# One-hots of the expert lookup in bfloat16 pairs, and the turn of the slot indices two pieces earlier

## The chip, the core and the metric

The kernel runs on one core of one Trainium2 chip, as one launch. Its time is device time in microseconds (us); the number compared is the median of repeated executions. Engines are named as the profile names them: PE (TensorE, matmuls; PEld its weight loads), DVE (VectorE), ACT (ScalarE), POOL (GpSimd), SP (which only issues DMAs here).

## The reference

Two transformer blocks run one after the other over 256 tokens of width 1024. The change touches one part, the product-key expert layer (PEER) that stands twice in the first block. For each token and each of 8 heads it finds the 16 best of 128 keys on each of two sides, adds them in pairs, keeps the 16 best pairs, and from the place of each pair it looks up which two keys made it:

```python
s = jnp.einsum('bthcd,hcnd->bthcn', q, sub_keys).astype(F32)
top_s, top_i = lax.top_k(s, PEER_TOPK)                       # 16 of 128, for both sides c
cand_s = (top_s[..., 0, :, None] + top_s[..., 1, None, :]).reshape(B, T, PEER_HEADS, -1)
cand_i = (top_i[..., 0, :, None] * PEER_NKEYS + top_i[..., 1, None, :]).reshape(B, T, PEER_HEADS, -1)
best_s, pos = lax.top_k(cand_s, PEER_TOPK)                   # 16 of 256 pairs
idx = jnp.take_along_axis(cand_i, pos, axis=-1)
gate = jax.nn.softmax(best_s, axis=-1)
...
h = jax.nn.gelu(jnp.einsum('md,mkd->mk', xb, exp_u[ib]), approximate=False)
return jnp.einsum('mk,mkd->md', (gb * h).astype(xb.dtype), exp_v[ib])
```

All 16384 experts are computed for all tokens by the kernel, and a table of gates (zero where an expert was not chosen) weighs them.

## The kernel before

All engines run programs written out by hand and meet at counted semaphores; the order within an engine is the order of the code. The expert layer (functions `peer_tensor`, `peer_scalar`, `peer_vector`, `load_peer`, once for each of the two layers) has 64 "pieces" of 256 experts, in two phases.

In the first phase, the h phase, piece c is 48 matmuls on PE (lines 1389 to 1391: two halves of 8 steps with three passes each, so that fp32r halves add up to full precision). Its weights come in raw by DMA; ACT rounds each half (`split_u`, L1539), DVE subtracts the rounded from the raw half (`residue_u`, L1634, two instructions of 128x1024 for a piece), and PE needs both. There are four buffers of half a piece, so DVE and ACT can be at most two pieces ahead of PE: the second residue of piece c waits for ACT, which waits until PE is through with piece c - 2. After each piece ACT applies the gelu (L1547), and after every fourth it also issues a store (L1550).

Beside this work, DVE chooses the experts, in stretches between residues. `between(work)` adds up given costs and puts in the two residues of the next piece when 24 is reached, and then counts from 0 again. First come the searches for the 16 best (L1651 to L1660). Then, four times (two token tiles n // 2, two sides n % 2), a one-hot of 128 pairs x 16 places is compared (L1689), multiplied by the 16 key numbers (L1693) and summed over the 16 places (L1695), all in fp32; that yields `slotI` and `slotJ`. Then the gates `slotG` are made (L1699 to L1701), one more piece of residues is put out, and DVE waits for PE to turn the three arrays (`turn_slots`, six transposes, L1454, which PE does after piece `SLOTS_AT` = 30). DVE copies the turned values as bfloat16 pairs (L1706 to L1713).

From piece `GATES_FROM` = 32 to `GATES_TO` = 60, 32 "groups" of 8 tokens are spread over the pieces by `groups_at`: DVE builds one-hots for a group (`one_hots`, five instructions of 128x1024 bfloat16, L1725 to L1730, in which each value stands twice in neighbouring places), PE multiplies them (24 matmuls, L1465), ACT copies the result out (L1559), and every fourth group is stored. With 28 pieces for 32 groups, pieces 32, 39, 46 and 53 have two groups. Before the groups of piece c, DVE has put out the residues of all pieces up to c + 1. The second phase, the y phase, begins when the gates have been stored and read back.

Of the kernel before, what the change touches and what calls it, by code (L numbers as in the profile page):

```python
# [7 lines left out]
ALU = mybir.AluOpType  # L8
ACT = mybir.ActivationFunctionType
AXX = mybir.AxisListType.X  # L10
F32 = mybir.dt.float32
U32 = mybir.dt.uint32
I32 = mybir.dt.int32
F32R = mybir.dt.float32r
BF16 = mybir.dt.bfloat16


P = 128
T = 256
TT = T // P  # L20
# [14 lines left out]
TOPK = 16  # L35
# [104 lines left out]
def two_blocks(nc, x, mem, consts, cols, rows, small, subk, wfix, peer, moe, gtab, ctab, kvtab, out):  # L140
# [23 lines left out]
    def A(off, *shape):  # L164

        n = 1
        for d in shape:
            n *= d
        v = arena[:, off:off + n]
        if len(shape) == 2:  # L170
            return v.rearrange("p (a b) -> p a b", a=shape[0])
        if len(shape) == 3:
            return v.rearrange("p (a b c) -> p a b c", a=shape[0], b=shape[1])
        return v
# [6 lines left out]
    def K(name, *shape):  # L181
        o, n = CONST[name]
        v = con[:, o:o + n]
        return v.rearrange("p (a b) -> p a b", a=shape[0]) if len(shape) == 2 else v
# [21 lines left out]
    def over(ap, axis, n):  # L206

        v = ap.unsqueeze(axis)
        s = list(v.shape)
        s[axis] = n  # L210
        return v.to_broadcast(s)

    def along(ap, n):

        return over(ap, len(ap.shape), n)
# [6 lines left out]
    def S(name):  # L222
        if name not in sems:
            sems[name] = nc.alloc_semaphore(name)
        return sems[name]
# [58 lines left out]
    def link(ins):  # L284

        dve_steps[0] += 1
        ins.then_inc(S("dve_step"), 1)
        nc.vector.wait_ge(S("dve_step"), dve_steps[0])
# [977 lines left out]
    s_sb = A(0, TT, 16, NKEYS)  # L1266
    cand = A(4096, TT, 8, 256)
    qTp = A(8192, 8, T)
    tv, ti, tif = A(10240, TT * 16, TOPK), A(10752, TT * 16, TOPK).bitcast(U32), A(11264, TT * 16, TOPK)
    bv, bp = A(11776, TT * 8, TOPK), A(12032, TT * 8, TOPK).bitcast(U32)  # L1270
    pa, pb = A(12288, TT, P), A(12544, TT, P)
    pau, pbu = (A(o, TT, P).bitcast(U32) for o in (15616, 15872))
    oneh = [A(12800, P, TOPK), A(4096, P, TOPK)]
    slotI, slotJ, slotG = (A(o, TT, P) for o in (14848, 15104, 15360))
    gsum = A(16128, TT * 8)
    slots_of = [A(16384 + 256 * n, T).bitcast(BF16).rearrange("p (t q) -> p t q", q=2) for n in range(4)]
# [3 lines left out]
    iota16 = A(23552, 64).bitcast(BF16).rearrange("p (k q) -> p k q", q=2)  # L1280
# [89 lines left out]
    BLOCK = JG // JC  # L1370
    NB = 4

    EXP_AT, SLOTS_AT, GATES_FROM, GATES_TO = 23, 30, 32, 60
    MEMORY_AT = 20

    def groups_at(c):
# [240 lines left out]
    def peer_vector(dve, l):  # L1617
# [10 lines left out]
        def residue_u():  # L1628

            nonlocal done  # L1630
            for j in range(JC):
                m = JC * (hb + done) + j
                dve.wait_ge(S("w1_hi"), m + 1)
                dve.tensor_tensor(u_lo[m % NB], u_raw(done, j), u_hi[m % NB].bitcast(F32), ALU.subtract)\  # L1634
                   .then_inc(S("w1_lo"), 1)
            done += 1

        def between(work):

            nonlocal spent  # L1640
            spent += work
            if spent >= 24:
                residue_u()
                spent = 0
# [20 lines left out]
        for tt in range(TT):  # L1665
# [1 line left out]
            w = slice(16 * tt, 16 * tt + 16)  # L1667
            top16(lambda i: s_sb[:, tt, i, :], tv[:, w], ti[:, w], 16, 2)
            dve.sem_inc(S("keys_best"), 1)
        link(dve.tensor_copy(tif, ti))  # L1670
        between(6)
        for tt in range(TT):
            w = slice(8 * tt, 8 * tt + 8)
# [6 lines left out]
        link(dve.tensor_scalar(pbu, bpf, TOPK - 1, None, ALU.bitwise_and))  # L1680
        dve.tensor_tensor(bv, bv, along(gsum, TOPK), ALU.subtract).then_inc(S("gate_in"), 1)
        known = done
        dve.tensor_copy(pa, pau)
        link(dve.tensor_copy(pb, pbu))
        between(12)

        tif5 = tif.rearrange("p (a c h) k -> p a c h k", a=TT, c=2)
        for n in range(4):
            link(dve.tensor_tensor(oneh[n % 2], along((pa, pb)[n % 2][:, n // 2, :], TOPK),  # L1689
                                   over(K("iota")[:, 0:TOPK], 1, P), ALU.is_equal))  # L1690
            between(16)
            o4 = oneh[n % 2].rearrange("p (h k) a -> p h k a", h=8)
            link(dve.tensor_tensor(o4, o4, over(tif5[:, n // 2, n % 2], 2, TOPK), ALU.mult))  # L1693
            between(16)
            link(dve.tensor_reduce((slotI, slotJ)[n % 2][:, n // 2, :], oneh[n % 2], AXX, ALU.add))  # L1695
            between(16)
        assert known - 1 <= EXP_AT <= done, (known, done)
        dve.wait_ge(S("gate_exp"), l + 1)
        link(dve.tensor_reduce(gsum, bv, AXX, ALU.add))  # L1699
# [5 lines left out]
        dve.wait_ge(S("slots_mm"), l + 1)  # L1705
        dve.tensor_copy(I2, along(ps[:, 6, 0:T], 2))  # L1706
        dve.tensor_copy(J2, along(ps[:, 6, T:2 * T], 2))
        dve.tensor_copy(iota16, K("iota").rearrange("p (k q) -> p k q", q=2))
        link(dve.tensor_copy(G1, along(ps[:, 7, 0:T], 2)))
        link(dve.tensor_tensor(g_left, ps[:, 7, 0:T], G1[:, :, 0], ALU.subtract))  # L1710
        link(dve.tensor_copy(G2, along(g_left, 2)))
# [1356 lines left out]
    with block_ctx as block:  # L3068
# [48 lines left out]
        @block.vector  # L3117
        def _(dve):
            even_vector(dve)
            peer_vector(dve, 0)  # L3120
            odd_vector(dve)
            peer_vector(dve, 1)
            mix2_vector(dve)
            xa_vector(dve)
            moe_vector(dve)
# [93 lines left out]
```

## Time and profile before

| | us |
|---|---|
| median of 3 executions | 3217.57 |
| lowest, highest | 3216.59, 3219.06 |
| profiled execution, device time | 3216.88 |
| span in its trace | 3215.1 |
| PE busy | 3012.1 (94%) |
| DVE busy | 2201.4 (68%) |
| ACT busy | 1496.7 (47%) |

The span is the time from the first to the last instruction in the trace; 1.8 us of the device time lie around it. Busy time counts instructions of an engine that overlap once. The two expert layers lie at about 340 to 1160 and 1364 to 2180 us.

### The profile page before, as it was taken

To read this page: it belongs to the slowest core of one execution; us is meant where nothing else is said; L and a number is where in the kernel's file an instruction comes from. 1 tells how busy PE (TensorE), PEld (TensorE's weight loads), DVE (VectorE), ACT (ScalarE), POOL (GpSimd) and SP (SyncE) were. 2 spreads that over 40 slices of the span, in tenths; PEclk is the share of its full clock that TensorE was granted. 3 is DMA by queue.
4 is the path that set the end of the run, shared out by engine and by line. 5 is a ranking of instruction groups with operands and counts; after the bars stand their busy time and mean duration, and the time that the engine had idled before them with its cause. 6 is when DMAs were issued, how large, how long until landed. Compare 5 with 4: busy or idle time off the path is not lost.

```text
span 3215.1 us, 41793 instructions
## 1 busy us (share of the span) xinstructions
PE 3012.1 (94%) x17215; PEld 2494.8 (78%) x17215; DVE 2201.4 (68%) x3375; ACT 1496.7 (47%) x1736; POOL 60.1 (2%) x94
## 2 busy tenths in 40 slices
PE   8898999999999998899899999998997799999995
PEld 4785898999888856499899988876545578888884
DVE  0654698776676646379777666666723488999996
ACT  1220344665545411144466544443121278888884
POOL 0000000000000000000000000000000000000000
PEclk9897999999999999899999999998998799999998
DMA  6102465677988733246577897862233189999994
GB/s 233 42 1 90 146 236 199 226 261 287 368 290 292 261 144 118 105 168 224 193 261 252 320 347 282 296 232 79 105 131 131 59 341 394 403 399 394 400 394 184
DMA packets 111838, 746.55 MB, mean 232 GB/s; under 512 B 9200, under 2 KB 42272, under 8 KB 48800
## 3 DMA queue, kind: packets, MB, share of 16 engines
q1 hardware_dynamic: 96064, 640.68, 53.6%
q10 hardware_dynamic: 8256, 73.23, 5.5%
q0 software_dynamic: 7328, 29.97, 2.4%
q8 instruction: 136, 2.23, 0.3%
q14 instruction: 54, 0.44, 0.0%
HBM read 655.23 MB, written 88.60 MB: 231 GB/s over the span
## 4 chain that ended last, share of the span: by engine, by line
PE 86%; DVE 10%; DMA 2%; ACT 2%; issue 1%; ACTq 0%; SPq 0%; POOL 0%; DVEq 0%; POOLq 0%
PE ps L1389 19%; PE ps L1390 19%; PE ps L1391 19%; PE ps L396 10%; PE ps L390 7%; PE ps L1465 2%; PE ps L669 1%; DMA gate_table<-arena 1%; DVE ring_rounded L1634 1%; DVE rounded L1634 1%; DMA ring<-in_peer_dram 1%; DVE arena L1689 1%; DVE arena L1693 1%; DVE arena L1695 1%; PE ps L2729 0%
## 5 line engine op out<-in xcount | busy, mean ns | idle before, releaser
L1389 PE MATMUL ps<-rounded 128*128 128x512 f32 (+1 forms) x2048 | 692.9, 338 | 14.0 <-DVE rounded L1634 7.8
L1390 PE MATMUL ps<-rounded 128*128 128x512 f32 (+1 forms) x2048 | 689.8, 337 | 0.0
L1391 PE MATMUL ps<-rounded 128*128 128x512 f32 (+1 forms) x2048 | 689.6, 337 | 0.0
L2854 DVE TENSOR_TENSOR rounded<-ring,rounded 128x1024 fp32r<-128x1024 f32 x420 | 486.5, 1220 | 36.3 <-ACT rounded L2768 33.9
L1389 PEld LDWEIGHTS ps<-rounded 128*128 128x128 f32 x2048 | 390.2, 191 | 55.0 <-issue 10.6
L1390 PEld LDWEIGHTS ps<-rounded 128*128 128x128 f32 x2048 | 390.4, 191 | 39.9
L1391 PEld LDWEIGHTS ps<-rounded 128*128 128x128 f32 x2048 | 390.3, 191 | 40.0
L2768 ACT CAST rounded<-ring 128x1024 fp32r<-128x1024 f32 x420 | 408.8, 1047 | 16.9 <-DMA ring<-in_moe_dram 13.6
L1752 DVE TENSOR_TENSOR rounded<-ring,rounded 128x1024 fp32r<-128x1024 f32 x256 | 313.7, 1225 | 83.7 <-ACT rounded L1573 83.5
L1573 ACT CAST rounded<-ring 128x1024 fp32r<-128x1024 f32 x256 | 268.2, 1049 | 144.9 <-PE ps L1391 129.3
L1389 PE MATMUL ps<-rounded,ring_rounded 128*128 128x256 f32 x1024 | 292.6, 286 | 14.0 <-DVE ring_rounded L1634 12.5
L1391 PE MATMUL ps<-rounded,ring_rounded 128*128 128x256 f32 x1024 | 290.2, 283 | 0.0
L1390 PE MATMUL ps<-rounded,ring_rounded 128*128 128x256 f32 x1024 | 289.3, 283 | 0.0
L1389 PE MATMUL ps<-rounded,xT_rounded 128*128 128x512 f32 x560 | 226.0, 404 | 7.7 <-ACT xT_rounded L2774 5.3
L390 PE MATMUL ps<-xT,ring 128*128 128x256 f32 (+3 forms) x960 | 218.3, 390 | 7.1 <-ACT xT L349 3.7
L1390 PE MATMUL ps<-rounded,xT_rounded 128*128 128x512 f32 x560 | 222.4, 397 | 0.0
L1391 PE MATMUL ps<-rounded,xT_rounded 128*128 128x512 f32 x560 | 221.2, 395 | 0.0
L390 PEld LDWEIGHTS ps<-xT,ring 128*128 128x128 f32 (+3 forms) x960 | 183.2, 192 | 42.4 <-issue 8.7
L1634 DVE TENSOR_TENSOR ring_rounded<-ring,ring_rounded 128x1024 fp32r<-128x1024 f32 x128 | 155.9, 1231 | 78.7 <-ACT ring_rounded L1539 78.3
L1389 PEld LDWEIGHTS ps<-rounded,ring_rounded 128*128 128x128 f32 x1024 | 194.7, 190 | 15.1 <-issue 11.0
L1390 PEld LDWEIGHTS ps<-rounded,ring_rounded 128*128 128x128 f32 x1024 | 194.7, 190 | 0.0
L1391 PEld LDWEIGHTS ps<-rounded,ring_rounded 128*128 128x128 f32 x1024 | 193.2, 189 | 0.0
(577 smaller groups left out, 4397.1 us busy)
## 6 DMA issues: line engine op xcount, KB each, us to landing
ring<-in_peer_dram SPq DMA_DIRECT2D x256, 1024.0 KB, 5.6
ring<-in_moe_dram SPq DMA_DIRECT2D x105, 2048.0 KB, 12.2
ring<-in_wfix_dram SPq DMA_DIRECT2D x39, 2048.0 KB, 7.6
hidden_table<-ring ACTq DMA_DIRECT2D x32, 1024.0 KB, 4.5
gate_table<-arena ACTq DMA_DIRECT2D x16, 2048.0 KB, 11.3
arena<-gate_table SPq DMA_DIRECT2D x32, 1024.0 KB, 8.2
arena<-hidden_table SPq DMA_DIRECT2D x32, 1024.0 KB, 10.4
expert_rows<-lnrow POOLq DMA_DIRECT2D x35, 512.0 KB, 6.9
```

The costliest lines, as they stand in the source:

```text
L390: last = pe.matmul(ps[0:n, b, o:o + T], w[:, k, c0:c0 + n], rhs[:, k, :], start=(k == 0), stop=(k == kd - 1))
L396: last = pe.matmul(ps[:, b, 0:n], lhs[:, k, tt * P:(tt + 1) * P], w[:, k, c0:c0 + n], start=(k == 0), stop=(k == kd - 1))
L669: last = pe.matmul(ps[:, b, o:o + P], left[:, p, tt, :], right[:, p, tt, :], start=True, stop=True)
L1389: pe.matmul(dst, lh, rh, start=start, stop=False, **kw)
L1390: pe.matmul(dst, lh, rl_, start=False, stop=False, **kw)
L1391: return pe.matmul(dst, ll, rh, start=False, stop=stop, **kw)
L1465: last = pe.matmul(ps[:, 2 + 2 * u + t // 4, t % 4 * P:(t % 4 + 1) * P], ohI[u][:, t].rearrange("p k q -> p (k q)"), part[u][:, t].rearran ...
L1573: act.copy(v_hi[m % NB], v_raw(c, j)).then_inc(S("w2_hi"), 1)
L1634: dve.tensor_tensor(u_lo[m % NB], u_raw(done, j), u_hi[m % NB].bitcast(F32), ALU.subtract)\
L1752: dve.tensor_tensor(v_lo[m % NB], v_raw(c, j), v_hi[m % NB].bitcast(F32), ALU.subtract).then_inc(S("w2_lo"), 1)
L2768: act.copy(w_hi[m % NUNIT], unit_raw(m)).then_inc(S("mo_hi"), 1)
L2854: dve.tensor_tensor(w_lo[m % NUNIT], unit_raw(m), w_hi[m % NUNIT].bitcast(F32), ALU.subtract)\
```

## The change

The one-hots, the key numbers and the places in the list of pairs are held in bfloat16 (numbers below 128 are exact in it). The two places `pa` and `pb` are written twice in neighbouring elements, as the comparison's table `iota16` has them. The 16 products are first added in halves of 8 (bfloat16, one of the two is zero) and then summed. The costs given to `between` are smaller (10, 10, 13 for each round where they were 16, 16, 16). `iota16` is made earlier. `SLOTS_AT` is 28 where it was 30, `GATES_FROM` 30 where it was 32; with 30 pieces for 32 groups, pieces 30 and 45 have two groups.

```diff
-    tv, ti, tif = A(10240, TT * 16, TOPK), A(10752, TT * 16, TOPK).bitcast(U32), A(11264, TT * 16, TOPK)
+    tv, ti = A(10240, TT * 16, TOPK), A(10752, TT * 16, TOPK).bitcast(U32)
+    ti16 = A(11264, 256).bitcast(BF16).rearrange("p (a c h k) -> p a c h k", a=TT, c=2, h=8)
-    pa, pb = A(12288, TT, P), A(12544, TT, P)
+    pa, pb = (A(o, 256).bitcast(BF16).rearrange("p (a x q) -> p a x q", a=TT, q=2) for o in (12288, 12544))
-    oneh = [A(12800, P, TOPK), A(4096, P, TOPK)]
+    oneh = [A(o, 1024).bitcast(BF16).rearrange("p (x a) -> p x a", a=TOPK) for o in (12800, 4096)]
...
-    EXP_AT, SLOTS_AT, GATES_FROM, GATES_TO = 23, 30, 32, 60
+    EXP_AT, SLOTS_AT, GATES_FROM, GATES_TO = 23, 28, 30, 60
...
-        link(dve.tensor_copy(tif, ti))
+        dve.tensor_copy(iota16, K("iota").rearrange("p (k q) -> p k q", q=2))
+        link(dve.tensor_copy(ti16, ti.rearrange("p (a c h) k -> p a c h k", a=TT, c=2)))
...
-        dve.tensor_copy(pa, pau)
-        link(dve.tensor_copy(pb, pbu))
+        dve.tensor_copy(pa, along(pau, 2))
+        link(dve.tensor_copy(pb, along(pbu, 2)))
         between(12)
 
-        tif5 = tif.rearrange("p (a c h) k -> p a c h k", a=TT, c=2)
         for n in range(4):
-            link(dve.tensor_tensor(oneh[n % 2], along((pa, pb)[n % 2][:, n // 2, :], TOPK),
-                                   over(K("iota")[:, 0:TOPK], 1, P), ALU.is_equal))
-            between(16)
-            o4 = oneh[n % 2].rearrange("p (h k) a -> p h k a", h=8)
-            link(dve.tensor_tensor(o4, o4, over(tif5[:, n // 2, n % 2], 2, TOPK), ALU.mult))
-            between(16)
-            link(dve.tensor_reduce((slotI, slotJ)[n % 2][:, n // 2, :], oneh[n % 2], AXX, ALU.add))
-            between(16)
+            o = oneh[n % 2]
+            link(dve.tensor_tensor(o.rearrange("p x (a q) -> p x a q", q=2), over((pa, pb)[n % 2][:, n // 2], 2, TOPK // 2),
+                                   over(iota16[:, 0:TOPK // 2], 1, P), ALU.is_equal))
+            between(10)
+            o4 = o.rearrange("p (h k) a -> p h k a", h=8)
+            link(dve.tensor_tensor(o4, o4, over(ti16[:, n // 2, n % 2], 2, TOPK), ALU.mult))
+            between(10)
+            link(dve.tensor_tensor(o[:, :, 0:8], o[:, :, 0:8], o[:, :, 8:16], ALU.add))
+            link(dve.tensor_reduce((slotI, slotJ)[n % 2][:, n // 2, :], o[:, :, 0:8], AXX, ALU.add))
+            between(13)
...
-        dve.tensor_copy(iota16, K("iota").rearrange("p (k q) -> p k q", q=2))
```

First place: DVE, the lookup, from the residues of piece 23 on. L1634 are the two residues of one piece; L1689, L1693 and L1695 are compare, multiply and sum. The kernel before:

```order
267 L1634 TENSOR_TENSOR ring_rounded<-ring,ring_rounded 128x1024 x2
268 L1689 TENSOR_TENSOR arena<-arena,con 128x2048
269 L1693 TENSOR_TENSOR arena<-arena 128x2048
270 L1634 TENSOR_TENSOR rounded<-ring,rounded 128x1024 x2
271 L1695 TENSOR_REDUCE arena<-arena 128x128
272 L1689 TENSOR_TENSOR arena<-arena,con 128x2048
273 L1634 TENSOR_TENSOR ring_rounded<-ring,ring_rounded 128x1024 x2
```

The changed kernel at the same place (L1635 are the residues; L1691, L1695, L1697 and L1698 are compare, multiply, add of halves and sum):

```order
268 L1635 TENSOR_TENSOR ring_rounded<-ring,ring_rounded 128x1024 x2
269 L1691 TENSOR_TENSOR arena<-arena 128x2048
270 L1695 TENSOR_TENSOR arena<-arena 128x2048
271 L1697 TENSOR_TENSOR arena<-arena 128x128x8
272 L1698 TENSOR_REDUCE arena<-arena 128x128
273 L1635 TENSOR_TENSOR rounded<-ring,rounded 128x1024 x2
274 L1691 TENSOR_TENSOR arena<-arena 128x2048
275 L1695 TENSOR_TENSOR arena<-arena 128x2048
```

Before, two lookup instructions stand between the residues of one piece and the next, so that the twelve of them carry the residues of six pieces (24 to 29). Now a whole round of four stands between them, and the four rounds carry those of four pieces (24 to 27).

Second place: DVE around its wait for the turned arrays, the end of the lookup and what follows, in the kernel before (L1699 to L1701 make the gates, L1706 on are the copies behind the wait):

```order
285 L1634 TENSOR_TENSOR ring_rounded<-ring,ring_rounded 128x1024 x2
286 L1699 TENSOR_REDUCE arena<-arena 128x16
287 L1700 RECIPROCAL arena<-arena 128x16
288 L1701 TENSOR_TENSOR arena<-arena 128x256
289 L1634 TENSOR_TENSOR rounded<-ring,rounded 128x1024 x2
290 L1706 CAST arena<-ps 128x512
291 L1707 CAST arena<-ps 128x512
292 L1708 CAST arena<-con 128x128
293 L1709 CAST arena<-ps 128x512
```

The changed kernel (L1709 is the first copy behind the wait):

```order
288 L1635 TENSOR_TENSOR ring_rounded<-ring,ring_rounded 128x1024 x2
289 L1702 TENSOR_REDUCE arena<-arena 128x16
290 L1703 RECIPROCAL arena<-arena 128x16
291 L1704 TENSOR_TENSOR arena<-arena 128x256
292 L1635 TENSOR_TENSOR rounded<-ring,rounded 128x1024 x2
293 L1709 CAST arena<-ps 128x512
294 L1710 CAST arena<-ps 128x512
295 L1711 CAST arena<-ps 128x512
```

Row 289 before holds the residues of piece 30, row 292 of the changed kernel those of piece 28; in both, the residues of the piece behind the turn come after the copies. The copy of `iota16` (L1708) is gone from behind the wait.

## Rows read from the trace of the kernel before

**Rows 1.** The page: the chain that ended last, by engine
```profile
PE 86%; DVE 10%; DMA 2%; ACT 2%; issue 1%; ACTq 0%; SPq 0%; POOL 0%; DVEq 0%; POOLq 0%
```

**Rows 2.** Busy time by stretch (us, instructions), first layer, then granted clock, DMA
```profile
494.00:535.00 41.00, 38.40 (x317) 37.87 (x316) 40.59 (x25) 21.03 (x24) 0.00 (x0) 1.00 0.58 205
535.00:560.00 25.00, 19.70 (x154) 19.49 (x154) 13.37 (x19) 6.80 (x9) 0.00 (x0) 0.93 0.46 164
```

**Rows 3.** Timeline of PE, h phase of the first layer: every start after idling
```profile
520.69 0.36 PE L1389 MATMUL ps<-rounded,ring_rounded 128*128 128x256 f32 x1 [0.75 <-ACT ring L1547]
527.61 0.36 PE L1389 MATMUL ps<-rounded 128*128 128x256 f32 x1 [0.92 <-DVE rounded L1634]
534.52 0.36 PE L1389 MATMUL ps<-rounded,ring_rounded 128*128 128x256 f32 x1 [0.94 <-DVE ring_rounded L1634]
...
546.10 0.82 PE L1454 MATMUL ps<-con,arena 128*128 128x128 f32 x6
552.22 0.55 PE L1389 MATMUL ps<-rounded,ring_rounded 128*128 128x256 f32 x1 [5.30 <-DVE ring_rounded L1634]
```

**Rows 4.** Timeline of PE, the groups: starts after idling, first layer
```profile
565.94 1.51 PE L1465 MATMUL ps<-arena 128*128 128x128 bf16 x24 [0.65 <-DVE arena L1730]
568.95 0.73 PE L1465 MATMUL ps<-arena 128*128 128x128 bf16 x10 [1.50 <-DVE arena L1730]
...
620.95 0.23 PE L1465 MATMUL ps<-arena 128*128 128x128 bf16 x1 [0.38 <-DVE arena L1730]
```

**Rows 5.** Timeline of PE, second layer: the longest of the same starts
```profile
1576.14 0.55 PE L1389 MATMUL ps<-rounded,ring_rounded 128*128 128x256 f32 x1 [5.31 <-DVE ring_rounded L1634]
```

**Rows 6.** Timeline of DVE, lookup and turn, first layer
```profile
491.53 2.48 DVE L1634 TENSOR_TENSOR ring_rounded<-ring,ring_rounded 128x1024 fp32r<-128x1024 f32 x2
493.92 2.28 DVE L1689 TENSOR_TENSOR arena<-arena,con 128x2048 f32<-128x2048 f32 x1
...
498.56 2.36 DVE L1634 TENSOR_TENSOR rounded<-ring,rounded 128x1024 fp32r<-128x1024 f32 x2
500.84 2.28 DVE L1695 TENSOR_REDUCE arena<-arena 128x128 f32<-128x2048 f32 x1
...
519.32 2.36 DVE L1634 TENSOR_TENSOR ring_rounded<-ring,ring_rounded 128x1024 fp32r<-128x1024 f32 x2
...
535.43 0.41 DVE L1699 TENSOR_REDUCE arena<-arena 128x16 f32<-128x256 f32 x1
...
536.51 2.35 DVE L1634 TENSOR_TENSOR rounded<-ring,rounded 128x1024 fp32r<-128x1024 f32 x2
546.96 0.69 DVE L1706 CAST arena<-ps 128x512 bf16<-128x512 f32 x1 [8.10 <-PE ps L1454]
...
548.16 0.22 DVE L1708 CAST arena<-con 128x128 bf16<-128x128 f32 x1
548.30 0.68 DVE L1709 CAST arena<-ps 128x512 bf16<-128x512 f32 x1
```

**Rows 7.** Timeline of DVE, first one-hots of a group, first layer
```profile
561.64 1.23 DVE L1634 TENSOR_TENSOR ring_rounded<-ring,ring_rounded 128x1024 fp32r<-128x1024 f32 x1 [2.59 <-ACT ring_rounded L1539]
562.78 0.69 DVE L1725 TENSOR_TENSOR arena<-arena 128x1024 bf16<-128x1024 bf16 x1
563.39 0.69 DVE L1726 TENSOR_TENSOR arena<-arena 128x1024 bf16<-128x1024 bf16 x1
```

**Rows 8.** Timeline of ACT: gelus of pieces 25, 26 and 31
```profile
514.22 0.60 ACT L1547 ACTIVATE ring<-ps 128x512 f32<-128x512 f32 x1 [1.76 <-PE ps L1391]
514.72 1.04 ACT L1539 CAST ring_rounded<-ring 128x1024 fp32r<-128x1024 f32 x1
...
519.98 0.60 ACT L1547 ACTIVATE ring<-ps 128x512 f32<-128x512 f32 x1 [1.77 <-PE ps L1391]
...
559.57 0.60 ACT L1547 ACTIVATE ring<-ps 128x512 f32<-128x512 f32 x1 [1.77 <-PE ps L1391]
...
560.56 1.05 ACT L1539 CAST ring_rounded<-ring 128x1024 fp32r<-128x1024 f32 x1 [0.40 <-ACT ring L1547]
```

## The prediction

> **What bounds the kernel now.** I looked first at the chain that ended last: 86% of it is PE, 10% DVE [rows 1]. So something moves the time only if it lets PE start earlier, and the question is where PE idles near the edited code. The table of busy time by stretch shows that place. While DVE does the lookup (494 to 535 us) it is busy 40.59 of 41 us and PE only 38.40; in the next 25 us, around the turn, PE is busy 19.70 [rows 2]. The timeline of PE then gives each start after idling. In the h phase of the first layer, up to the first group, these are four: 0.75, 0.92 and 0.94 us before pieces 27, 28 and 29, and 5.30 us behind the turn (which began at 546.10) before piece 31 [rows 3]. The first of them is put down to ACT's gelu, but the residue it needs came out of DVE at 519.32 + 1.2, 0.15 us before PE started at 520.69 [rows 3, 6]: it too is DVE's. From there on PE idles only at the pieces with two groups: 0.65 and 1.50 at piece 32, and 0.38 at each of 39, 46 and 53, which all read alike (one is shown) [rows 4]. The second layer repeats it 1023.9 us later, its turn costing 5.31 [rows 5]. What the change can give back is thus 2.61 + 5.30 + 2.15 + 1.14 = 11.2 us in a layer, and no more.
>
> **Why PE waits in the lookup.** A piece takes PE 5.76 us (gelus at 514.22 and 519.98) [rows 8]. DVE puts two lookup instructions between residues: 4.64 us from 493.92 to 498.56, and 2.28 for the residues themselves (498.56 to 500.84), so 6.92 a piece [rows 6]. It falls behind by 1.16 a piece, uses up a lead of two pieces, and from piece 27 on PE waits.
>
> **The lookup, new.** No lookup instruction in bfloat16 stands in the trace, but the comparison of a group has the same form (pairs against a repeated table): 0.69 for 1024 elements [rows 7]. In fp32, 1024 elements take 1.23 and 2048 take 2.28 [rows 6, 7], so 0.18 of an instruction is fixed. The group's takes 0.51 above that, and 2048 elements would take 0.18 + 2 x 0.51 = 1.20. A result that is waited for adds 0.04 (4.64 for two instructions of 2.28). I take 1.24 each for comparison and multiplication, and 0.73 for the add of halves (1024 elements). The sum over 8 places reads 1024 bfloat16 elements; its bounds are 0.73, if it is as fast as the group's instructions, and 1.27, if it runs as an fp32 one of that size. I take 1.27, since the old sum was no faster than the fp32 comparison (2.28 both) [rows 6]. A round is 1.24 + 1.24 + 0.73 + 1.27 = 4.48, with one piece of residues 6.76.
>
> The Trainium skill says the same of that sum: by its page "VectorE: DVE Perf Modes", section "The perf-mode tier table", `tensor_tensor` doubles its rate in bfloat16 and `tensor_reduce` does not. No run of before has a sum in bfloat16. By that rule the round stays 4.48; were it wrong, it would be 3.94.
>
> Now the lateness of each piece. The residues of piece 23 start at 491.53 [rows 6]; writing `pa` and `pb` twice makes them 512 elements, for which I take 0.3 more together (the 128x1024 fp32 residue takes 1.23, so 256 elements more on each cost at most 0.27 at that rate), of which 0.1 goes into a wait for ACT that stands there (the pair took 2.48 and not 2.36). The first lookup starts at 494.12 and not 493.92. The residues of 24 follow at 498.6, of 25 at 505.3, of 26 at 512.1, of 27 at 518.9 (494.12 + 4 x 4.48 + 3 x 2.28). The first half of piece 27 is ready at 518.9 + 1.35 = 520.2; PE is through with piece 26 at 519.94, 0.04 before its gelu [rows 8]. It waits 0.3. The gates then take 1.08 (535.43 to 536.51) [rows 6], the residues of 28 start at 522.3, and PE wants them at 525.9: no wait. So 2.61 becomes 0.3: **2.3 saved**. The copies of `iota16` and of the key numbers stand much earlier, where DVE waits for ACT anyway between searches; up to about a microsecond there costs nothing.
>
> **The turn.** `SLOTS_AT` falls by two, but so does the number of pieces whose residues are out by then: the lookup carries four and not six. In the order, one piece of residues stands between the gates and the wait, before and after. So PE still turns with nothing in hand, and waits for DVE's copies and the residues of piece 29. The stall moves two pieces forward and stays, less the `iota16` copy: 548.16 to 548.30 [rows 6], **0.14 saved**.
>
> **The half clock.** Behind the turn PE's first matmul takes 0.55 where the others after a short wait take 0.36 [rows 3], and the granted clock of the stretch is 0.93 [rows 2]: 0.07 x 25 x 2 = 3.5 us at 1.2 GHz and not 2.4, which costs at most 1.75. An idle time of about the same length moves to another moment. Bounds: the slow part goes away (1.75 gained a layer), or lasts twice as long (1.75 lost). I take no change, since both layers show the same (5.30 and 5.31).
>
> **The groups.** The first two groups: their one-hots start behind the second residue of piece 33, which waits for ACT's rounding after the gelu of piece 31. That gelu is followed by a store (every fourth piece), so the rounding came 560.56 - 559.57 = 0.99 after it; without a store it is 514.72 - 514.22 = 0.50 [rows 8]. After the change the same place is the gelu of piece 29, with no store: both groups are **0.5 earlier**, 2.15 of idling becomes 1.65. Pieces with two groups: one more (45) in place of three more, 2 x 0.38 = **0.76 saved**. The last four groups are at pieces 56 to 59 as before, so the y phase starts from the same point. PE's own work is unchanged: 48 matmuls a piece, 768 for the groups.
>
> **Sum.** 2.3 + 0.14 + 0.5 + 0.76 = 3.7 a layer, 7.4 for two. The profiled execution would be 3216.88 - 7.4 = 3209.5; it is 0.69 below the median of 3217.57, so the forecast in medians is 3217.57 - 7.4 = **3210.2**.
>
> **Rivals.** About 0.2% (6.4 us) is what a measurement of this kernel can tell from no change.
>
> *The half clock takes it back.* If the slow part behind the turn lasts up to twice as long in both layers, 3.5 goes: gain 3.9, 3213.7. For it: the turn's moment shifts by some 14 us against everything else. Against: equal in both layers before.
>
> *DVE stays as late.* If waits between linked instructions or 16-byte runs cost more, so that a round keeps the old 4.64 (0.04 more on each of four instructions), the residues of 27 come at 519.5 and PE waits 0.9; with 5.1 a round it waits 2.6 as now: gain 1.4 a layer, 3214.8. For it: DVE has no margin at piece 27. Against: the group's instructions, of the same form, read 0.69 each time.
>
> *Slower.* If compare and multiply in this layout run at one element a clock, as fp32 does, a round is 2.32 + 2.32 + 1.27 + 1.27 = 7.18. DVE is then far behind: residues of 27 start at 529.7, PE waits 11.1 and not 2.6, 8.5 lost against 1.4 gained: 7.1 a layer, 3231.8. It turns from gain to loss where a round takes 5.4 (PE waiting 4.0), slower by 0.2% from 6.2. Against it: the group's comparison has the same repeated pairs and ran at double rate [rows 7].
>
> *More than forecast.* The slow part goes away in both layers: 3.5 more, 3206.7; or the sum is fast: 0.6 more.
>
> **How the numbers follow.** Forecast 0.49 (6.5 to 9 us gained, 3208.5 to 3211), more than forecast 0.10, half clock 0.22, DVE as late 0.14, slower 0.05. The first two are faster, 0.59; the next two within 0.2%, 0.36; slower 0.05. The range takes the forecast, the half-clock case (together 0.71) and most of the larger gain: 3207 to 3213.8.
>
> **What would show it.** In the changed profile: L1691 and L1695 at about 1.2 us, L1697 0.7, L1698 1.2; residues 6.7 us apart in the lookup; PE idle some 0.3 before piece 27, none before 28; an idle of 5.1 to 5.2 behind the turn, beginning some 14 us earlier; two starts at piece 30 with together 1.65; one of 0.38 at piece 45. It is wrong if a round exceeds 4.7, if the half clock lasts other than 3.5 us behind the turn, or if the start of the y phase gives the gain back.

## The result, and the profile after

The median went from 3215.14 us to 3205.30 us (10 executions each); the ratio is 0.9964, interval 0.9955 to 0.9974. Forecast was 3210.2 from 3217.57, a ratio of 0.9977, with a range whose lower end was 3207: the direction held, but the gain was 10 (by the medians) to 12 us (by the ratio) and not 7.4. The median of before stood 2.4 us lower over ten executions than in the three that the forecast started from.

| us | before | after |
|---|---|---|
| span of the profiled execution | 3215.1 | 3204.9 |
| chain: PE, DVE | 86%, 10% | 87%, 9% |
| h phase, first layer (first matmul to first of the y phase) | 362.89 to 795.19: 432.30 | 364.42 to 793.60: 429.18 |
| h phase, second layer | 1385.79 to 1817.87: 432.08 | 1381.59 to 1809.23: 427.64 |
| all the rest | 2350.7 | 2348.1 |

The timeline of PE in the changed kernel, the same starts after idling as in [rows 3, 4] (start us, us, engine, line, operation, count, idle before and what ended it), with the two ends of the first h phase:

```profile
364.42 0.55 PE L1390 MATMUL ps<-rounded 128*128 128x256 f32 x1 [2.97 <-DVE rounded L1635]
...
522.84 0.36 PE L1390 MATMUL ps<-rounded,ring_rounded 128*128 128x256 f32 x1 [0.31 <-DVE ring_rounded L1635]
...
534.42 0.82 PE L1455 MATMUL ps<-con,arena 128*128 128x128 f32 x6
540.40 0.55 PE L1390 MATMUL ps<-rounded,ring_rounded 128*128 128x256 f32 x1 [5.17 <-DVE ring_rounded L1635]
...
553.98 1.51 PE L1466 MATMUL ps<-arena 128*128 128x128 bf16 x24 [0.15 <-DVE arena L1732]
556.99 0.23 PE L1466 MATMUL ps<-arena 128*128 128x128 bf16 x1 [1.50 <-DVE arena L1732]
...
666.28 0.23 PE L1466 MATMUL ps<-arena 128*128 128x128 bf16 x1 [0.38 <-DVE arena L1732]
...
793.60 0.76 PE L1390 MATMUL ps<-rounded 128*128 128x512 f32 x1 [2.50 <-DVE rounded L1759]
```

Three waits of together 2.61 us before pieces 27 to 29 have become one of 0.31; the 5.30 behind the turn are 5.17; the 0.65 at piece 32 are 0.15 at piece 30; the 1.50 stay; three waits of 0.38 are one. That is 3.7 us less idling, as counted. The second layer reads the same to 0.01 or 0.02 (0.30, 5.17, 0.14, 1.50, 0.38).

The timeline of DVE in the lookup of the changed kernel, against [rows 6]:

```profile
493.59 0.42 DVE L1685 CAST arena<-arena 128x512 bf16<-128x512 uint32 x1
493.93 0.42 DVE L1686 CAST arena<-arena 128x512 bf16<-128x512 uint32 x1
494.38 2.36 DVE L1635 TENSOR_TENSOR ring_rounded<-ring,ring_rounded 128x1024 fp32r<-128x1024 f32 x2
496.66 1.22 DVE L1691 TENSOR_TENSOR arena<-arena 128x2048 bf16<-128x2048 bf16 x1
497.91 1.23 DVE L1695 TENSOR_TENSOR arena<-arena 128x2048 bf16<-128x2048 bf16 x1
499.17 0.69 DVE L1697 TENSOR_TENSOR arena<-arena 128x1024 bf16<-128x1024 bf16 x1
499.90 1.22 DVE L1698 TENSOR_REDUCE arena<-arena 128x128 f32<-128x1024 bf16 x1
501.15 2.36 DVE L1635 TENSOR_TENSOR rounded<-ring,rounded 128x1024 fp32r<-128x1024 f32 x2
...
521.47 2.36 DVE L1635 TENSOR_TENSOR ring_rounded<-ring,ring_rounded 128x1024 fp32r<-128x1024 f32 x2
```

A round is 501.15 - 496.66 = 4.49 us (4.48 forecast). Compare and multiply with 2048 bfloat16 elements take 1.22 and 1.23, and the sum of 1024 takes 1.22: the sum runs at half their rate. This agrees with the Trainium skill's page "VectorE: DVE Perf Modes" (section "The perf-mode tier table").

The two h phases together take 864.38 us before and 856.82 after, 7.56 less. Of the 10.2 us by which the spans differ, 2.6 lie outside. Matmuls that take a different time in the two profiles stand, for one, in the odd mixer (a stage between the two expert layers), far from any edited line. The kernel before, timeline of PE:

```profile
1208.73 6.55 PE L1900 MATMUL ps<-arena 64*128 64x256 f32 x32 [2.12 <-DVE arena L2009]
1217.43 3.58 PE L297 MATMUL ps<-con,arena 128*128 128x128 f32 x16 [2.15 <-ACT arena L1965]
```

The changed kernel, the same matmuls:

```profile
1207.12 4.91 PE L1902 MATMUL ps<-arena 64*128 64x256 f32 x32 [2.12 <-DVE arena L2011]
1214.59 1.94 PE L297 MATMUL ps<-con,arena 128*128 128x128 f32 x16 [2.56 <-DVEq L2015]
```

The same work takes 1.64 us less each time, behind nearly the same idle times; the mean granted clock from 1190 to 1225 us is 0.90 before and 1.00 after. The table of busy time by stretch shows something alike for a longer one, the 840 matmuls of the second block's mixer from the first to the last (stretch, then its length, and busy us and count of PE, PEld, DVE, ACT and POOL; then granted clock, DMA share, GB/s). Before:

```profile
2187.00:2429.00 242.00, 237.79 (x840) 139.52 (x840) 129.86 (x261) 50.75 (x72) 0.00 (x0) 0.97 0.30 109
```

After:

```profile
2178.00:2416.00 238.00, 233.31 (x840) 136.79 (x840) 130.29 (x262) 51.24 (x73) 0.00 (x0) 0.99 0.30 111
```

PE is busy 4.5 us less with as many matmuls, and the mean granted clock is 0.99 and not 0.97. In one pair of executions either could be chance, so the question for the experiments was twofold: do the counted terms hold one by one, and is the rest chance or does it belong to the kernel?

### The profile page after: what moved, and what is told of

It is laid out like the page before. It is cut to its first block, busy times and chain, and to the rows that moved or that the text cites. A ratio compares the mean times of both kernels' runs of the same rounds, so it can differ in the third digit from the quotient of the medians.

```text
span 3204.9 us, 41797 instructions
## 1 busy us (share of the span) xinstructions
PE 3014.9 (94%) x17215; PEld 2497.9 (78%) x17215; DVE 2181.3 (68%) x3383; ACT 1498.0 (47%) x1736; POOL 60.1 (2%) x94
## 4 chain that ended last, share of the span: by engine, by line
PE 87%; DVE 9%; DMA 2%; ACT 1%; issue 1%; ACTq 0%; POOL 0%; SPq 0%; DVEq 0%; POOLq 0%
PE ps L1390 20%; PE ps L1391 19%; PE ps L1392 19%; PE ps L396 10%; PE ps L390 7%; PE ps L1466 2%; PE ps L669 1%; DMA gate_table<-arena 1%; DVE ring_rounded L1635 1%; DVE rounded L1635 1%; DMA arena<-hidden_table 0%; PE ps L2731 0%; DMA con<-in_consts_dram 0%; PE ps L1431 0%; PE ps L2147 0%
## 5 line engine op out<-in xcount | busy, mean ns | idle before, releaser
L2856 DVE TENSOR_TENSOR rounded<-ring,rounded 128x1024 fp32r<-128x1024 f32 x420 | 486.4, 1220 | 49.4 <-ACT rounded L2770 47.1
L1754 DVE TENSOR_TENSOR rounded<-ring,rounded 128x1024 fp32r<-128x1024 f32 x256 | 313.8, 1226 | 83.2 <-ACT rounded L1574 82.9
L1635 DVE TENSOR_TENSOR ring_rounded<-ring,ring_rounded 128x1024 fp32r<-128x1024 f32 x128 | 156.5, 1235 | 85.8 <-ACT ring_rounded L1540 85.6
L1390 PEld LDWEIGHTS ps<-rounded,ring_rounded 128*128 128x128 f32 x1024 | 195.2, 191 | 11.7 <-issue 11.7
L1391 PEld LDWEIGHTS ps<-rounded,ring_rounded 128*128 128x128 f32 x1024 | 195.0, 190 | 0.0
L1635 DVE TENSOR_TENSOR rounded<-ring,rounded 128x1024 fp32r<-128x1024 f32 x128 | 155.4, 1231 | 58.1 <-ACT rounded L1540 57.5
```

Of the source, the lines that this page charges most:

```text
L1390: pe.matmul(dst, lh, rh, start=start, stop=False, **kw)
L1391: pe.matmul(dst, lh, rl_, start=False, stop=False, **kw)
L1754: dve.tensor_tensor(v_lo[m % NB], v_raw(c, j), v_hi[m % NB].bitcast(F32), ALU.subtract).then_inc(S("w2_lo"), 1)
L2856: dve.tensor_tensor(w_lo[m % NUNIT], unit_raw(m), w_hi[m % NUNIT].bitcast(F32), ALU.subtract)\
```

## The experiments

The median of the kernel before was 3215.59 (23 executions) beside the first four runs below, 3216.03 (9) beside the next four, 3215.69 (27) beside the third four and 3214.67 (17) beside the last four. "h phases" is the sum of both from the profile of each run.

| version | h phases | median | ratio to before, interval |
|---|---|---|---|
| kernel before, three profiles | 864.38, 865.65, 864.07 | 3214.67 to 3216.03 | |
| changed kernel, three profiles | 856.82, 857.11, 857.50 | 3205.30, 3205.92 | 0.9964, 0.9962 (0.9949 to 0.9975) |
| lookup alone | 858.94 | 3210.54 | 0.9981 (0.9971 to 0.9991) |
| changed, groups from 32 | 860.26 | 3213.15 | 0.9993 (0.9983 to 1.0002) |
| changed, two ahead | 842.83 | 3192.81 | 0.9923 (0.9909 to 0.9936) |
| before, two ahead | 850.37 | 3202.19 | 0.9961 (0.9947 to 0.9975) |
| two ahead, even groups | 839.64 | 3199.44 | 0.9944 (0.9930 to 0.9957) |

**The changed kernel again** (no edit).

> The changed kernel once more. Theory A (idle ledger and half clock): the edited places save 3.7 us of PE idling in each layer, 7.4 in all, and whatever the total shows beyond that comes from where PE's stretches at 1.2 GHz fall, which differs from run to run; so the idle rows in the two h phases repeat to 0.05 us (0.31, 5.17, 1.50, 0.38), and the rest of the trace moves by up to 4 us against the first profile, mostly in stretches that hold no edited line. Time 0.9965 to 0.998 of the kernel before. Theory B (the edit gives more than the ledger): the surplus of some 3 us sits at the same places again, the start of the y phase of the first layer above all, and the ratio is 0.9964 again.

The idle rows came out as 0.30, 5.17, 0.16, 1.50 and 0.38, the h phases as 429.22 and 427.89, and the ratio as 0.9962. The counted part repeats (theory A). So does the ratio, with the surplus in it, as theory B had it, but not at the place that B named: the start of the y phase idled 2.46 us against 2.50 in the first profile of the changed kernel and 2.65 in that of before.

**The lookup alone.** The residues are put out as often as before, turn and groups stand where they stood (the first `between` line stands twice):

```diff
-    EXP_AT, SLOTS_AT, GATES_FROM, GATES_TO = 23, 28, 30, 60
+    EXP_AT, SLOTS_AT, GATES_FROM, GATES_TO = 23, 30, 32, 60
...
-            between(10)
+            between(16)
-            between(13)
+            between(16)
```

> The bfloat16 lookup alone: old costs between residues (16, 16, 16), turn after piece 30, groups from 32. Theory A: DVE is never late in the lookup (two short instructions and a piece of residues take about 4.8 us against PE's 5.76), so the 2.61 us before pieces 27 to 29 go; the turn costs 5.17; the groups idle 2.15 and 1.14 as before. 2.7 us a layer, 5.5 in all: 0.9983 of the kernel before. Theory B (all of the gain is the faster lookup, the move of turn and groups gives nothing): 0.9964.

No idling before pieces 27 to 29, 5.17 behind the turn, then 0.66, 1.50 and three of about 0.38. The h phases are 5.44 us shorter than in the first profile of before (5.5 expected), and the ratio 0.9981 (0.9983). DVE even has to wait again in the lookup, for ACT:

```profile
501.62 1.23 DVE L1635 TENSOR_TENSOR rounded<-ring,rounded 128x1024 fp32r<-128x1024 f32 x1
503.55 1.23 DVE L1635 TENSOR_TENSOR rounded<-ring,rounded 128x1024 fp32r<-128x1024 f32 x1 [0.71 <-ACT rounded L1540]
```

So the faster lookup, with its residues put out as often as before, is worth 2.7 us a layer (2.61 of idling and 0.13 behind the turn). Cut as in the changed kernel it is worth 0.3 less, the wait that stays before piece 27.

**Groups from 32.**

```diff
-    EXP_AT, SLOTS_AT, GATES_FROM, GATES_TO = 23, 28, 30, 60
+    EXP_AT, SLOTS_AT, GATES_FROM, GATES_TO = 23, 28, 32, 60
```

> The changed kernel with its 32 groups spread from piece 32 and not 30, the turn after piece 28 as changed. Theory A: four pieces have two groups again; DVE reaches the first group with time in hand (two more pieces without groups since the turn), so that the first group still idles little and the second 1.1 to 1.5, and three later ones idle 0.38 each: 0.8 to 1.3 us a layer more than the changed kernel, about 2.0 in all, 0.9970 to 0.9982 of the kernel before. Rival (spreading gives nothing): the same time as the changed kernel.

The idle rows are 0.66 and 1.50 at piece 32 and 0.38 to 0.40 at three later ones, so two more pieces without groups give DVE no time in hand. The h phases are 3.15 us longer than in the changed kernel's second profile, against 2 expected and 2.6 by its idle rows. But the whole is 7.2 us slower than the changed kernel, and not told apart from the kernel before (the interval ends at 1.0002): the time came out higher than expected, by some 4 us that no idle row of the h phases holds. The first group's 0.66 also shows what its 0.15 in the changed kernel hangs on. Turn and lookup are as in the changed kernel, and only the piece of the first groups differs: for piece 32 the gelu of piece 31 counts, which a store follows, for piece 30 that of piece 29, which none does.

**Two ahead.** DVE puts out two pieces of residues before it waits for the turned arrays:

```diff
         assert done - 2 <= SLOTS_AT <= done, done
         residue_u()
+        residue_u()
         dve.wait_ge(S("slots_mm"), l + 1)
```

> The changed kernel with the residues of two pieces, not one, put out by DVE before it waits for the turned arrays. Theory A: PE has piece 29 in hand behind the turn (5.76 us) while DVE copies (3.9) and makes the first residue of piece 30 (1.2), so the idle time of 5.17 behind the turn is gone, and with it the stretch at half clock (up to 1.75 more): 5.2 to 6.9 us a layer, 10 to 14 less than the changed kernel, 0.992 to 0.9935 of the kernel before. The first groups idle 1.65 as in the changed kernel. Rival (the wait only moves): DVE, now later by one piece of residues, becomes late at the first groups and gives back more than 3 us a layer; then the ratio is 0.995.

The timeline of PE around the turn of this version:

```profile
534.24 0.82 PE L1455 MATMUL ps<-con,arena 128*128 128x128 f32 x6
534.81 0.36 PE L1390 MATMUL ps<-rounded,ring_rounded 128*128 128x256 f32 x1
535.01 0.28 PE L1391 MATMUL ps<-rounded,ring_rounded 128*128 128x256 f32 x1
...
549.71 0.45 PE L1466 MATMUL ps<-arena 128*128 128x128 bf16 x5 [1.50 <-DVE arena L1733]
```

And of DVE there:

```profile
530.75 1.23 DVE L1635 TENSOR_TENSOR ring_rounded<-ring,ring_rounded 128x1024 fp32r<-128x1024 f32 x1 [2.59 <-ACT ring_rounded L1540]
535.09 0.69 DVE L1710 CAST arena<-ps 128x512 bf16<-128x512 f32 x1 [3.11 <-PE ps L1455]
```

PE goes on at once, at full speed (0.36 and not 0.55), DVE waits 3.1 us for the turn and not 8.1, and the first groups idle no more than before. The h phases are 14 us shorter than the changed kernel's, 7 a layer: 5.2 of idling and some 1.8 of half clock (an estimate, the difference of the two). With a median of 3192.81 and 0.9923 it is the fastest version tried, and faster than both kernels.

**The same on the kernel before.**

> The kernel before (fp32 lookup, turn after piece 30, groups from 32) with the residues of two pieces instead of one put out before DVE waits for the turned arrays. Theory A: the 2.61 us before pieces 27 to 29 stay, the 5.30 behind the turn go and its half clock with them (up to 1.75): 5.3 to 7 us a layer, 10.6 to 14 in all, 0.9957 to 0.9967 of the kernel before. It tells how much of the gain of the two-ahead version rests on the bfloat16 lookup: by theory A none of this part. Rival (with the slow lookup DVE has no time for a further piece, and PE waits at the first groups instead): less than 6 us in all, 0.998 or more.

0.9961, and h phases 13.7 us shorter than in the third profile of before. The waits before pieces 27 to 29 stand as in [rows 3] (0.75, 0.92, 0.93). The extra piece needs none of the bfloat16 lookup; by itself it gives as much by the ratio as the whole change under study (0.9961 against 0.9962 and 0.9964), and nearly twice as much in the h phases.

**Is the surplus there in every profile?** Before twice more, and the changed kernel a third time.

> The kernel before once more, for a second profile. What is asked: does what the changed kernel gained beyond the counted 7.4 us sit in the edited stages or outside them? Theory A (outside, where stretches at 1.2 GHz fall): the two h phases take 432.3 and 432.1 us again (from the first matmul to the first of the y phase, within 1 us), the rest of the span differs by 1 to 4 us from the first profile. Theory B (the edited stages gain more than counted): in a second profile the h phases of before are longer than 432.3, by 1 us or more each.

> The kernel before a third time, for the same question as the second: by theory A h phases of 432.3 and 432.1 within 1 us, the rest moving by 1 to 4 us between the three profiles; by theory B h phases that are longer by 1 us or more in some of them.

> The changed kernel a third time. Theory A: h phases of 429.2 and 427.8 within 1 us, as in its first two profiles (429.18, 427.64 and 429.22, 427.89), and a rest that moves by 1 to 4 us. Theory B: the h phases stay the same and the rest is shorter than that of before in each profile, by 2 us or more, at one and the same place.

For the h phases it is theory A, but for one value (433.42 in the second profile of before, 1.1 above 432.3 where 1 was allowed): the h phases of before repeat to 1.6 us and those of the changed kernel to 0.7; their means differ by 864.70 - 857.14 = 7.56. The rest of the span takes 2350.7, 2353.2 and 2346.5 in before and 2348.1, 2349.4 and 2347.0 after: 2.0 less in the mean, with 6.6 between two profiles of the same kernel. PE's idle times in the second block read alike to 0.02 in all six (7.55, 8.30, 1.43, 14.05, 4.61 and others), all but one, which is 1.3 or 2.4. What moves is how long the matmuls between them take.

Three profiles each also tell chance from what repeats, place by place. The 364 us ahead of the first h phase, which no edit touches, take 362.3 to 367.3 us over all eighteen profiles: that much is chance. The odd mixer is chance too, for the third profile of before has the short form there and the second of the changed kernel the long one. The kernel before, third profile, timeline of PE:

```profile
1210.19 4.91 PE L1900 MATMUL ps<-arena 64*128 64x256 f32 x32 [2.12 <-DVE arena L2009]
```

The changed kernel, second profile:

```profile
1207.38 6.55 PE L1902 MATMUL ps<-arena 64*128 64x256 f32 x32 [2.12 <-DVE arena L2011]
```

The second block's mixer repeats. Its 840 matmuls take 238.3, 238.2 and 235.2 us from first to last in the three profiles of before, and 233.8, 233.6 and 233.6 in those of the changed kernel: 3.5 less in the mean. Some 80 us into it PE works through 48 small matmuls (128x32, L2170 or L2172) without idling, and at their end the clock falls to 1.2 GHz for a few us in every profile of before and in none of the changed kernel. The table of busy time by stretch, 80 to 95 us into that mixer (columns as above), the three profiles of before:

```profile
2267.53:2282.53 15.00, 15.00 (x64) 10.14 (x63) 14.68 (x35) 0.60 (x1) 0.00 (x0) 0.77 0.00 1
2267.33:2282.33 15.00, 15.00 (x64) 10.26 (x63) 14.68 (x35) 0.60 (x1) 0.00 (x0) 0.77 0.00 1
2266.03:2281.03 15.00, 15.00 (x62) 9.00 (x62) 14.71 (x34) 1.79 (x2) 0.00 (x0) 0.89 0.08 16
```

And of the changed kernel:

```profile
2258.88:2273.88 15.00, 15.00 (x68) 9.36 (x68) 14.72 (x35) 2.11 (x3) 0.00 (x0) 1.00 0.16 43
2261.79:2276.79 15.00, 15.00 (x67) 9.26 (x67) 14.72 (x35) 1.92 (x3) 0.00 (x0) 1.00 0.17 46
2259.92:2274.92 15.00, 15.00 (x67) 9.26 (x67) 14.72 (x35) 1.92 (x3) 0.00 (x0) 1.00 0.18 52
```

The whole rest does not follow theory B (2347.0 after stands above 2346.5 before), but this one place nearly does: it is shorter in each profile of the changed kernel than in each of before, by 1.3 us at least.

**Delays.** To see whether that depends on the kernel's timing, small copies (3, 7 or 10) were put where PE idles 7.55 us behind the second expert layer:

```diff
         for tt in range(TT):
             dve.wait_ge(S("y_tile"), TT * l + tt + 1)
+            if l == 1 and tt == 0:
+                for _ in range(3):
+                    link(dve.tensor_copy(iota16, K("iota").rearrange("p (k q) -> p k q", q=2)))
```

> The changed kernel with three small copies (128x128, about 0.25 us each with the wait) that DVE makes behind the last piece of the second expert layer, where PE idles 7.55 us for DVE in any case. They lengthen that idle time by some 0.75 us and change nothing else. Question: does the cost of half clock further down depend on when things start? Theory A1 (half clock falls at random, its mean does not depend on the program's timing): the time is 0.75 us above the changed kernel's, whatever the delay, within 2 us. Theory A2 (one stretch sets the moment of the next, so that a fixed shift moves the mean of all that follows): over the three delays of 0.75, 1.7 and 2.5 us the time less the delay is not constant, but moves by 3 us or more.

> As the run with three copies, with seven: the idle time before the second block is some 1.7 us longer. Theory A1: 1.7 us above the changed kernel's time, within 2 us. Theory A2: time less delay differs by 3 us or more from that of another of the delays or of the changed kernel.

> As the run with three copies, with ten: the idle time is some 2.5 us longer. Theory A1: 2.5 us above the changed kernel's time, within 2 us. Theory A2: time less delay differs by 3 us or more from that of another of the delays or of the changed kernel.

**Even groups.** The two-ahead version, with its first two groups at pieces 30 and 31:

```diff
-        return [g for g in range(GROUPS) if first + g * many // GROUPS == c]
+        return [g for g in range(GROUPS) if first + (g * many + GROUPS // 2) // GROUPS == c]
```

> The two-ahead version with the 32 groups spread so that piece 30 has one and not two (two now at pieces 38 and 54 only). The first group's 0.15 and the second's 1.50 us of idling become 0.15 and one more 0.38: 1.1 us a layer, 2.2 in all less than the two-ahead version (3192.8): 0.9916 of the kernel before. Rival (DVE has not the time for a group right behind the turn, and the wait moves to piece 31): the same as the two-ahead version.

Its PE idles only 0.40 and 0.38 in the groups, and its h phases are 419.96 and 419.68, 3.2 us shorter than those of the two-ahead version (the second pair of groups falls at piece 53, not 54). As a whole it is 6.6 us slower. The forecast of its time failed, and in no edited place: its profile has the second block's mixer at 237.6 us, where that of the two-ahead version has 233.9.

**Delays in other kernels**, the same three in the even version, and seven copies in the kernel before. "Moment theory" is A2 from above: the moment at which the later work starts decides what the half clock costs.

> The even two-ahead version (median 3199.4) with three small copies by DVE behind the second expert layer, 0.78 us more of idling for PE. By the moment theory the time less the delay differs from 3199.4 in either direction, by up to 4 us, and over the three delays of this version it goes up and down; one of them may be below 3199.4 although it idles more. By the rival (each us of idling there costs some 3.5 us, as 4, 6.4 and 9 us for the three delays of the changed kernel): 3202 to 3203.

> As the run before with seven copies, 1.83 us more of idling. Moment theory: between 3197 and 3204, and not in line with the other two delays. Rival: 3205 to 3207.

> As the run before with ten copies, 2.61 us more of idling. Moment theory: between 3198 and 3205. Rival: 3208 to 3210.

> The kernel before with seven copies at the same place, 1.83 us more of idling. Moment theory: 3214 to 3221, since its later work starts at another moment than the changed kernel's; a cost of the delay below 1.8 us or none would speak for it. Rival: 6 us more than the kernel before, 3221 to 3223.

PE's idle time before the second block is 7.55 us in the even version and 9.38 with seven copies. The even version, timeline of PE:

```profile
2152.15 0.69 PE L321 MATMUL ps<-con,arena 128*128 128x128 f32 x2 [7.55 <-DVEq L1787]
```

With seven copies:

```profile
2149.74 1.97 PE L321 MATMUL ps<-con,arena 128*128 128x128 f32 x8 [9.38 <-DVEq L1790]
```

| copies | idle added | changed kernel: median, less idle added | even version: median, less idle added |
|---|---|---|---|
| 0 | 0 | 3205.3, 3205.3 | 3199.4, 3199.4 |
| 3 | 0.78 | 3209.2, 3208.4 | 3197.6, 3196.8 |
| 7 | 1.83 | 3211.7, 3209.8 | 3195.3, 3193.5 |
| 10 | 2.61 | 3214.3, 3211.7 | 3198.8, 3196.1 |

In the changed kernel the time less the idle added rises by 3.1, 4.5 and 6.4 us above 3205.3 (by 2.5, 3.9 and 5.8 above the other median, 3205.9), so half clock does not fall at random there (A2 and not A1): a delay of 2.6 us costs 9. In the kernel before, 1.8 us cost 8.5 (3223.14 against 3214.67; ratio 1.0024, 1.0015 to 1.0032), more than the 1.8 to 6.3 expected by the moment theory, and more than its rival's 6. In the even version the three delays cost nothing that can be told from noise: the ratios are 0.9946, 0.9939 and 0.9948 against 0.9944, all within one another's intervals. That a delay of 1.8 us gives something there (the medians say 4 us, of five and six executions in different sessions) is not shown; but the rival, by which each us of idling there costs some 3.5, falls with it, for it asked for 3208 to 3210 with ten copies, and 3198.8 was measured. What stays is that a small shift of the later work can cost up to some 6 us more than itself, and that how much belongs to the kernel.

The second block's mixer goes along with this. One profile of each version (three of before and of the changed kernel), the clock being that of the stretch 80 to 95 us into the mixer, as above:

| version | mixer, us | clock |
|---|---|---|
| kernel before | 238.3, 238.2, 235.2 | 0.77, 0.77, 0.89 |
| changed kernel | 233.8, 233.6, 233.6 | 1.00, 1.00, 1.00 |
| changed, two ahead | 233.9 | 1.00 |
| lookup alone; before, two ahead | 235.1; 235.1 | 0.89; 0.89 |
| changed, groups from 32 | 238.0 | 0.77 |
| changed with 3, 7, 10 copies | 238.2, 237.8, 237.4 | 0.77, 0.77, 0.77 |
| before with 7 copies | 237.5 | 0.77 |
| even version; with 3, 7, 10 copies | 237.6; 239.0, 235.2, 238.3 | 0.77; 0.66, 0.89, 0.77 |

All three delays bring back the slow stretch that the changed kernel is without, and with it some 4 us; moving the groups to piece 32 does so too, which is the size of what was missed there. Since each of these has one profile, the table shows where such a difference sits and not how often it does.

## Why the prediction was right, and where it was wrong

*Lookup, right.* A round 4.49 (4.48), the wait before piece 27 at 0.31 (0.3), none before 28 and 29. DVE and PE both came there about 2.6 us later than forecast (first lookup at 496.66 and not 494.12, PE through with piece 26 at 522.53 and not 519.94), which leaves the wait as it was. The higher bound for the sum was the right one to take.

*Turn, right.* It stays, at 5.17 (5.16): the smaller number of residues in the lookup cancels the smaller `SLOTS_AT`. The two-ahead versions confirm the reason, that PE turns with no piece in hand: with one in hand the idling is gone.

*Groups, right.* 0.65 became 0.15 at the first group, two waits of 0.38 went. The forecast put the 0.5 down to the store behind every fourth gelu, and the run with groups from 32 bears it out: 0.66 again.

*Half clock behind the turn: the mechanism wrong, the cost small, by luck.* "I take no change" did not hold. The table of busy time by stretch, first layer, while PE idles behind the turn and in the 5 us from its restart, before:

```profile
546.92:552.22 5.30, 0.00 (x0) 0.03 (x1) 5.09 (x10) 0.91 (x1) 0.00 (x0) 0.96 0.01 2
552.22:557.22 5.00, 5.00 (x31) 5.00 (x32) 3.26 (x3) 0.47 (x1) 0.00 (x0) 0.70 0.56 197
```

After:

```profile
535.23:540.40 5.17, 0.00 (x1) 0.03 (x1) 4.96 (x9) 0.91 (x1) 0.00 (x0) 0.71 0.01 2
540.40:545.40 5.00, 5.00 (x28) 5.00 (x28) 3.26 (x3) 0.11 (x1) 0.00 (x0) 0.62 0.60 203
```

The slow part is twice as long, some 6.8 us and not 3.4, in both layers and in all three profiles, which is the condition of the rival "the half clock takes it back" and a sign that the forecast itself had named as showing it wrong. But 3 us of it now fall while PE idles and cost nothing (clock 0.71 over 5.17 us). PE worked at 1.2 GHz for 3.8 us (0.62 over 5) and not 3.0 (0.70 over 5). From its restart to the end of its work before the first group it took 13.43 us and not 13.07 [rows 3, 4]: 0.36 a layer and 0.7 in all, where the rival had 3.5. Nothing in the forecast's argument kept it that small. The h phases still shortened by 7.56 where 7.4 was counted, because another small term stood against it: from the end of piece 26 to the restart PE takes 17.87 us, where before takes 20.76 when the two pieces of 5.76 that it has more there are taken off. That is 2.89 less, while the idle times there differ by 2.43, so each of the two waits that went cost some 0.2 more than its idle time.

*The sum, wrong.* The step that failed is "I take no change" for the half clock: its bounds were drawn only behind the turn, so that for the rest of the kernel this term stood at nothing, without a reason. Outside the h phases PE is at 1.2 GHz for a part of many stages (the granted clock is 0.91 over the first 362 us of before), and the later ones start 3 to 8 us earlier in the changed kernel. The runs show in its place a gain of 2.0 us outside the h phases in the mean of three profiles each; 2 us by the medians (9.8 and 9.7 less 7.56), and 4 by the ratios (11.6 and 12.2 less 7.56). Three profiles that differ by 6.6 among themselves could not show 2.0 alone. One place could: the second block's mixer is 3.5 us shorter in the mean, because a slow stretch at the end of its 48 small matmuls is in all three profiles of before and in none of the changed kernel. That a shift alone can change such a cost, the delays show, by up to 6.4 us; that it was the shift by 8 us which took this stretch away is argued from them and not shown by itself. The expected time thus had a further term of either sign. As an estimate its size is some 4 us, the 4.5 by which the mixer changes with that stretch, and the range should have reached about as far again on both sides: 3203 to 3218.

*The base, off.* The median of three executions was 3217.57; over more it is 3214.67 to 3216.03. Executions of before scatter from 3210 to 3226 us, where the three lay within 2.5. About half of the miss in absolute time (4.9 us) is this; from 3215.14 the same 7.4 would have given 3207.7, within the range.

*Rivals.* "The half clock takes it back" named the right quantity: its condition came true, at a fifth of its price, and the half clock decided the sum elsewhere, with the other sign. DVE stayed as late in no run with the new lookup, and nothing was slower.

Open: why a given shift brings the slow stretch into the second block's mixer in one version and not in another, and which stages hold the remainder. That would need many profiles of each version; most runs here give one.

## What to carry to other kernels

Count idle time of the bound engine place by place from the trace: here each idle time came out within 0.1 us, and the count showed the next step, one more piece of residues before a wait, worth 7 us a layer. A gain of a few us in a kernel whose PE drops to half clock in many stages is not decided by that count alone; try an unrelated delay too, take the scatter of executions from more than three, and compare several profiles of both kernels stage by stage: of two places that differed in the first pair here, one was chance and one was not. When a stall sits behind a wait, ask how many pieces the bound engine has in hand when the wait begins, before making the work behind it faster.

## What the runs showed of the hardware

A cast of 128x128 from fp32 to bfloat16 with each value doubled took DVE 0.22 us where POOL was idle (the `iota16` copy in [rows 6]) and 0.70 where it now stands, between the searches, when POOL begins its sums of pairs. Group of instructions by line, the changed kernel (count, min/median/max ns, first and last start):

```profile
L1671 DVE CAST arena<-con x2: 696/697/698, 434.5 to 1451.7; 128x128 bf16<-128x128 f32 x2
```

That POOL is the cause was not tried.

The TensorE clock can fall to 1.2 GHz while PE does not idle: it did so at the end of 48 matmuls of 128x32 in 14 of 18 profiles (granted clock 0.66 to 0.89 over the 15 us there, against 1.00 in the other four), and the stage with them took 1.3 to 5.2 us longer than the 233.8 us of the first profile without. A shift of the work ahead of it by a few us is enough to bring this in: 0.8 us of delay did, in the one profile taken.
